# A six-stage transformer kernel on one core: the last value slabs of each mixture layer summed tile by tile over a fourth pair of split buffers, and layer-norm squares centred by half rows

## The chip, the core and the metric

One core of one Trainium2 chip runs the whole program in one launch. The metric is the time on the device in microseconds (us), lower is better; the inputs are random data, batch 1, 256 tokens, width 1024, in f32.

## What is computed

Three mixers alternate with three product-key mixture layers (PEER). The first block (retention mixer, PEER, gated linear recurrence, PEER) closes each stage with a layer norm over a residual, the second (state-space mixer, PEER) with an RMS norm:

```python
h = layer_norm(DN_ALPHA * h + mix, ln_g[layer, 0], ln_b[layer, 0])
ffn = peer(h, peer_w_q[layer], peer_sub_keys[layer], peer_u[layer], peer_v[layer])
h = layer_norm(DN_ALPHA * h + ffn, ln_g[layer, 1], ln_b[layer, 1])
...
h = h + hybrid_mixer(rmsnorm(h, g_mix[l]), ...)
h = h + peer_ffn(rmsnorm(h, g_ffn[l]), ...)
h = rmsnorm(h, g_final)
```

A PEER layer has 16384 experts, of which each token takes 16 for each of 8 heads. The kernel does not gather them: it computes all experts densely, `gelu(x @ u)` times a gate matrix that is zero where an expert was not chosen, times `v`.

## The kernel before

The stages are `ab`, `peer0`, `c`, `peer1`, `s`, `peer2`. Every weight matrix is streamed in **slabs** of 128 x 1024 f32 (512 KB) through three ring buffers (`SLOTS = 3`). Each slab is split into a high and a low part in fp32r, so that three matmuls (high x high, low x high, high x low; L522 to L524, `split_matmuls`) give an f32 product:

- SyncE (`sync_program`, L341) issues the DMA of slab n+3 when the low part of slab n is done (`put`, L344).
- ScalarE copies the slab to `w_hi` (`split_lead`, L764, instruction at L772). It waits for `used`, the count of slabs that TensorE has finished: slab n overwrites the buffers of slab n-3.
- VectorE, in the second half of a PEER layer, or GpSimd elsewhere, computes `w_lo = ring - w_hi` (`split_rest`, L476, instruction at L479).
- TensorE uses it. In a "col" slab (`features`, L536) 24 matmuls of 256 columns produce 128 features in a `col` bank from the transposed input `x_hi`, `x_lo`. In a "row" slab (`rows`, L561) 12 matmuls of 512 columns add to the four banks `acc`, which hold 2 tiles of 128 tokens x 2 halves of 512 columns.

A PEER layer streams 16 query slabs, 128 `u` slabs (features of all experts) and 128 `v` slabs (the values, as rows). For a row slab ScalarE also writes the coefficients `c_hi` (`coef_lead`, L935, instruction at L937) and VectorE `c_lo` (`coef_rest`, L1175, instruction at L1179), again in three buffers. During the value slabs `x_hi` and `x_lo` hold nothing that is read.

**The end of a stage.** `row_tail` (L705) issues the last row slabs. The last but two goes as the others do, all four banks in turn. The last two go by tiles: tile 0 of both slabs, at which `tile_full` is raised; then the left half of tile 1 of both (`tile_full` again), then the right half (`used`). Meanwhile VectorE waits in `add_residual` (L1031), which adds `h` to a bank and, in a layer norm, also takes the sum of the half row. `layer_norm` (L1053) is a hand-written order on VectorE over tiles t and halves: residual, `minus_mean` (needs both halves' sums), `centre` (subtract the mean, times the gain), `variance`, reciprocal (`inverse_std`, L1046), `scale` (L1080; times the inverse deviation plus bias, to `h_tok`). ScalarE does the squares (`centred_squares`, L816; `square`, L826, instruction at L831, with the negated mean of the whole row as its bias), the square root (L814), and then, as TensorE transposes each scaled half (`transpose_x`, L573, 16 matmuls against the identity at L587), the copies to `x_hi` (`lead_x`, L801, L807); VectorE takes `x_lo` (`rest_x`, L1019, L1027). ScalarE's own order is in `finish` (L843), with the `split_lead` of the next stage's first three slabs (`end`, `end + 1`, `end + 2`) put between. The first column matmul of the next stage needs the first half of `x_lo` of both tiles. After `peer1` two norms follow each other, since `s` begins with an RMS norm; `norm_meta` (L1150) norms 16 extra rows before it. `finish_rms` (L1113) is the end of `s` and `peer2`.

## Time and profile before

| | |
|---|---|
| time of the runs, median of 3 | 3011.08 us (3005.74 to 3011.94) |
| time of the profiled execution | 3013.95 us |
| its span | 3012.2 us |
| mean granted TensorE clock | 0.988 of full speed |
| TensorE matmul busy | 2929.7 us (97%) |
| VectorE busy | 2103.5 us (70%) |
| ScalarE busy | 1575.1 us (52%) |
| GpSimd busy | 942.6 us (31%) |
| HBM | 506.05 MB read, 168 GB/s |

The span is that of one profiled execution, on one core; its own time is 1.75 us longer than its span. Engine names in the profile: PE is TensorE, PEld its weight loads, DVE VectorE, ACT ScalarE, POOL GpSimd, SP SyncE. A line such as L522 is a line of the kernel before. Matmuls overlap, so their pitch, from one start to the next, tells more than their length. "[5.00 <-DVE h_tok L1080]" says that the engine sat idle for 5.00 us before the instruction, and that what it waited for was written by VectorE at L1080.

### The profile page before, as it was taken

The page shows a single profiled execution, that of the slowest core. Times are in us where ns is not written, and L with a number is a line of the kernel's source. Part 1 is how long each engine was busy: PE and PEld are TensorE (multiplying, and loading weights), DVE is VectorE, ACT ScalarE, POOL GpSimd, SP SyncE. Part 2 cuts the span into 40 slices and gives each one's busy share as a digit, 9 for nine tenths or more (in the row PEclk, how much of TensorE's full clock was granted, in tenths as well). Part 3 has the DMA queues.
Part 4 walks back from the last instruction along what each step waited for, and adds up shares of the span by engine and source line. Part 5 has one row for each costly group of instructions (what it writes and reads, how often), then busy time and mean ns, then how long its engine had stood idle before and what let it go on. Part 6 is the DMA issues. An engine that isn't in the chain of part 4 may idle for free.

```text
span 3012.2 us, 66185 instructions
## 1 busy us (share of the span) xinstructions
PE 2929.7 (97%) x22893; PEld 2668.0 (89%) x22893; DVE 2103.5 (70%) x4319; ACT 1575.1 (52%) x2604; POOL 942.6 (31%) x378
## 2 busy tenths in 40 slices
PE   7899999999999989999999999899999999999999
PEld 6799999888888879999998888788799999988887
DVE  4369588888655654958888865675629668788755
ACT  3444444577555544454457754553644544477654
POOL 5589600000003757980000000155779810000000
PEclk9999999999999999999999999999999999999999
DMA  5455555555654435555555565444555555555554
GB/s 190 141 169 186 179 165 161 167 166 166 219 191 162 152 112 171 184 183 160 166 163 166 166 213 196 147 131 123 156 172 180 184 168 165 164 165 166 185 193 162
DMA packets 142993, 508.68 MB, mean 169 GB/s; under 512 B 17168, under 2 KB 18192, under 8 KB 142880
## 3 DMA queue, kind: packets, MB, share of 16 engines
q1 hardware_dynamic: 142880, 507.16, 52.4%
q8 instruction: 72, 1.18, 0.2%
q14 instruction: 41, 0.34, 0.0%
HBM read 506.05 MB, written 1.05 MB: 168 GB/s over the span
## 4 chain that ended last, share of the span: by engine, by line
PE 89%; DVE 5%; POOL 2%; ACT 2%; issue 1%; DMA 1%; SPq 0%; DVEq 0%; ACTq 0%; POOLq 0%
PE col L522 15%; PE col L524 15%; PE col L523 15%; PE acc L522 12%; PE acc L524 12%; PE acc L523 12%; POOL w_lo L479 2%; PE acc L645 2%; PE col L645 2%; ACT w_hi L772 1%; PE acc L605 1%; DMA ring<-in_ab_in 1%; DVE work L1838 0%; DVE work L1546 0%; DVE work L2294 0%
## 5 line engine op out<-in xcount | busy, mean ns | idle before, releaser
L479 POOL TENSOR_TENSOR w_lo<-ring,w_hi 128x1024 fp32r<-128x1024 f32 x374 | 942.4, 2530 | 1482.9 <-ACT w_hi L772 1481.8
L772 ACT ACTIVATE w_hi<-ring 128x1024 fp32r<-128x1024 f32 x941 | 993.7, 1056 | 556.9 <-PE acc L524 454.5
L522 PE MATMUL col<-x_hi,w_hi 128*128 128x256 f32 (+1 forms) x3976 | 1133.3, 285 | 10.8 <-DVE x_lo L1027 7.0
L523 PE MATMUL col<-x_lo,w_hi 128*128 128x256 f32 (+1 forms) x3976 | 1122.6, 282 | 0.0
L524 PE MATMUL col<-x_hi,w_lo 128*128 128x256 f32 (+1 forms) x3976 | 1121.5, 282 | 0.0
L479 DVE TENSOR_TENSOR w_lo<-ring,w_hi 128x1024 fp32r<-128x1024 f32 x567 | 693.2, 1223 | 261.7 <-ACT w_hi L772 260.6
L522 PEld LDWEIGHTS col<-x_hi,w_hi 128*128 128x128 f32 x3976 | 754.5, 190 | 16.5 <-issue 11.4
L524 PEld LDWEIGHTS col<-x_hi,w_lo 128*128 128x128 f32 x3976 | 755.5, 190 | 0.0
L523 PEld LDWEIGHTS col<-x_lo,w_hi 128*128 128x128 f32 x3976 | 751.9, 189 | 0.7
L522 PE MATMUL acc<-w_hi,c_hi 128*128 128x512 f32 x1664 | 660.8, 397 | 9.4 <-DVE c_lo L1172 5.3
L524 PE MATMUL acc<-w_hi,c_lo 128*128 128x512 f32 x1664 | 650.1, 391 | 0.0
L523 PE MATMUL acc<-w_lo,c_hi 128*128 128x512 f32 x1664 | 648.8, 390 | 0.0
L779 ACT ACTIVATE work<-col 128x256 f32 (+1 forms) x464 | 178.8, 385 | 775.1 <-PE col L524 774.9
L522 PEld LDWEIGHTS acc<-w_hi,c_hi 128*128 128x128 f32 x1664 | 313.3, 188 | 74.9 <-DVE c_lo L1172 6.6
L524 PEld LDWEIGHTS acc<-w_hi,c_lo 128*128 128x128 f32 x1664 | 313.0, 188 | 67.4
L523 PEld LDWEIGHTS acc<-w_lo,c_hi 128*128 128x128 f32 x1664 | 313.7, 189 | 62.5
L1298 DVE TENSOR_TENSOR gated_onehot_i<-mask_i,pairs_of_gate 128x768 bf16<-128x768 bf16 x384 | 227.9, 594 | 12.3
L1179 DVE TENSOR_TENSOR c_lo<-work,c_hi 128x256 fp32r<-128x256 f32 x387 | 163.7, 424 | 1.6 <-ACT c_hi L937 1.5
L937 ACT ACTIVATE c_hi<-work 128x256 fp32r (+1 forms) x384 | 153.4, 401 | 5.9 <-DVE work L1308 5.9
L1186 DVE MAX8 work<-work 128x8 f32<-128x128 f32 (+1 forms) x144 | 35.4, 322 | 168.4 <-ACT work L893 168.1
L1288 DVE TENSOR_TENSOR mask_i<-iota_bf,pairs_of_i_i 128x256 bf16<-128x256 bf16 x384 | 121.3, 316 | 44.5 <-DVE gated_onehot_i L1298 41.7
L1308 DVE TENSOR_TENSOR work<-work,acc 128x256 f32 (+1 forms) x192 | 73.9, 421 | 100.3 <-PE acc L645 55.4
(287 smaller groups left out, 2099.9 us busy)
## 6 DMA issues: line engine op xcount, KB each, us to landing
ring<-in_u SPq DMA_DIRECT2D x384, 512.0 KB, 3.5
ring<-in_v SPq DMA_DIRECT2D x384, 512.0 KB, 3.6
ring<-in_wq SPq DMA_DIRECT2D x48, 512.0 KB, 3.5
ring<-in_s_in SPq DMA_DIRECT2D x21, 512.0 KB, 3.6
ring<-in_c_in SPq DMA_DIRECT2D x16, 512.0 KB, 3.5
ring<-in_s_out SPq DMA_DIRECT2D x16, 512.0 KB, 3.6
ring<-in_s_gate SPq DMA_DIRECT2D x12, 512.0 KB, 3.5
ring<-in_s_conv SPq DMA_DIRECT2D x12, 512.0 KB, 3.6
```

Of the source, the lines that this page charges most:

```text
L479: eng.tensor_tensor(k.w_lo[s.slot][:, :], k.ring[s.slot][:, :], k.w_hi[s.slot][:, :].bitcast(F32), ALU.subtract).then_inc(k.lo[s.slot], 1)
L522: pe.matmul(out, a[0], b[0], start=start, stop=False, **kw)
L523: pe.matmul(out, a[0], b[1], start=False, stop=False, **kw)
L524: return pe.matmul(out, a[1], b[0], start=False, stop=stop, **kw)
L645: ins = pe.matmul(banks[b.slot][:, t * EARLY:(t + 1) * EARLY], k.oh1[:, b.base % 2, t, :], k.oh2[:, b.base % 2, n, t, :], start=n == 0, st ...
L772: act.activation(k.w_hi[s.slot][:, :], k.ring[s.slot][:, :], ACT.Copy).then_inc(k.hi[s.slot], 1)
L779: act.activation(dst, src, func).then_inc(k.evac, 1)
L937: act.activation(k.c_hi[s.slot][:, :], act_of[:, s.index(values), :], ACT.Copy).then_inc(k.coef_h, 1)
L1179: dve.tensor_tensor(k.c_lo[s.slot][:, :], src, k.c_hi[s.slot][:, :].bitcast(F32), ALU.subtract).then_inc(k.coef[s.slot], 1)
L1288: dve.tensor_tensor(mask, pairs[:, at // 2:(at + EARLY) // 2, :].unsqueeze(1).to_broadcast(shape), k.i2[:, tokens, :].unsqueeze(2).to_broa ...
L1298: dve.tensor_tensor(k.oh2[:, slot, :, :, :].rearrange("p n t (i two) -> p n t i two", two=2), mask.unsqueeze(1).to_broadcast(shape), k.gat ...
L1308: dve.tensor_tensor(part, part, banks[b.slot][:, 0:GB * EARLY].rearrange("p (t i) -> p i t", t=GB), ALU.mult).then_inc(k.g_used, 1)
```

## The change

Four things are changed.

1. **Buffers.** In each PEER layer the last 12 value slabs (`DEEP`) use four pairs of split buffers: the three `w_hi`/`w_lo` and a fourth in `x_hi`/`x_lo`. A slab there overwrites that of four before it. ScalarE and VectorE split slab n+1 ahead of the coefficients of slab n; the last slab's coefficients go to a further piece of `x_hi`/`x_lo`.
2. **Tail.** In a PEER layer the last four slabs go by tiles (`LONG`) and no longer the last two: tile 0 of all four, then the left half of tile 1 of all four, then the right half. At the end of a mixer it is two slabs as before (`SHORT`).
3. **Squares.** ScalarE squares each half row about the half's own mean, so that it needs the sum of that half alone. VectorE corrects the variance by the distance of the two half means, with two more small instructions for a tile (`mean` has two where `minus_mean` had one, and there is `apart`).
4. **Order.** `layer_norm`, `finish_rms` and `finish` are written in another order: tile 0 is brought to its scaled rows earlier, and the residual of tile 1's right half comes behind that in a PEER layer. `mean_square` has one instruction where it had two; RMS_EPS is the bias of the square root.

```diff
+SHORT, LONG = 2, 4
+DEEP = 3 * LONG
...
+    def open_deep(self):
+        self.w_home, self.w_before, self.c_home = {}, {}, {}
+        spare = [t[:, :, :].rearrange("p c t -> p (c t)") for t in (self.x_hi, self.x_lo)]
...
+            homes = [[t[:, 0:D] for t in spare]] + [[self.w_hi[n % SLOTS][:, :], self.w_lo[n % SLOTS][:, :]]
+                                                    for n in range(deep - SLOTS, deep)]
+            for n in range(DEEP):
+                self.w_home[deep + n] = homes[n % LONG]
+                self.w_before[deep + n] = deep + n - LONG if n else None
+            self.c_home[end - 1] = [t[:, D:D + T] for t in spare]
...
     def row_tail(self, end, count):
+        tail = [Slab(n) for n in range(end - count, end)]
...
+        for s in tail:
+            pe.wait_ge(k.coef[s.slot], k.rows_in_slot(s, 1))
+            self.slab_ready(s)
             for half in range(2):
+                ins = part(s, 0, half)
         ins.then_inc(k.tile_full, 1)
+        for s in tail:
+            ins = part(s, 1, 0)
+        ins.then_inc(k.tile_full, 1)
+        for s in tail:
+            part(s, 1, 1).then_inc(k.used, 1)
...
     def split_lead(self, s):
+        if s.turn is None and s.base in k.w_home:
+            if k.w_before[s.base] is not None:
+                act.wait_ge(k.used, k.w_before[s.base] + 1)
+        elif s.turn is not None or s.base >= SLOTS:
             act.wait_ge(k.used, s.index(SLOTS - 1))
...
     def finish(self, name, end):
+        deep = name[:4] == "peer"
...
+        if not deep:
+            self.split_lead(Slab(end))
+        for half in range(2):
+            self.centred_square(0, half)
+        self.tile_std(0, eps)
+        self.centred_square(1, 0)
+        if deep:
+            self.split_lead(Slab(end))
         if after != ("s",):
+            if deep:
+                self.split_lead(Slab(end + 1))
+                self.lead_x([0], halves=[0])
+                self.centred_square(1, 1)
+                self.tile_std(1, eps)
+                self.lead_x([0], halves=[1])
+            else:
+                self.centred_square(1, 1)
+                self.split_lead(Slab(end + 1))
+                self.tile_std(1, eps)
+                self.lead_x([0])
             self.lead_x([1])
             self.split_lead(Slab(end + 2))
         else:
+            self.tile_squares(0)
+            self.split_lead(Slab(end + 1))
+            self.centred_square(1, 1)
             self.tile_std(1, eps)
             self.lead_meta()
+            self.tile_squares(1)
+            self.split_lead(Slab(end + 2))
             self.lead_x(range(NT), at=META)
...
     def peer(self, layer):
+        self.split_lead(Slab(values + deep - 1))
+        for n in range(deep - 1, KEYS):
+            if n + 1 < KEYS:
+                self.split_lead(Slab(values + n + 1))
             coef_lead(Slab(values + n))
...
     def layer_norm(self, slot, last, rms_next, deep):
         residual(0, 0)
         residual(0, 1)
-        minus_mean(0)
-        residual(1, 0)
+        mean(0)
         centre(0, 0)
-        residual(1, 1)
-        minus_mean(1)
+        apart(0)
+        if not deep:
+            residual(1, 0)
         centre(0, 1)
         variance(0)
-        centre(1, 0)
-        centre(1, 1)
-        variance(1)
-        own.join()
+        residual(1, 0 if deep else 1)
+        if not deep:
+            mean(1)
         self.inverse_std(0)
         scale(0, 0)
         scale(0, 1)
+        if rms_next:
+            self.mean_square(0, squared + 5)
+        if deep:
+            residual(1, 1)
+            mean(1)
+        if rms_next:
+            self.inverse_std(0)
+        centre(1, 0)
+        apart(1)
+        variance(1)
+        centre(1, 1)
+        own.join()
         self.inverse_std(1)
         scale(1, 0)
+        scale(1, 1)
...
     def finish_rms(self, name, last):
+        residual(0, 0)
+        residual(0, 1)
+        if not deep:
+            residual(1, 0)
+        self.mean_square(0, squared + 2)
+        if not deep:
+            residual(1, 1)
+        self.inverse_std(0)
+        self.rms_norm(0, slot)
+        if deep:
+            residual(1, 0)
+            residual(1, 1)
+        self.mean_square(1, squared + 4)
+        self.inverse_std(1)
+        self.rms_norm(1, slot)
```

The order of instructions on VectorE at the end of `peer0`, from the last coefficients on, before:

```order
L1179 TENSOR_TENSOR c_lo<-work,c_hi 128x256
L1039 SCALAR_TENSOR_TENSOR acc,small<-h_tok,acc 128x512 x2
L1063 TENSOR_SCALAR small<-small 128x1
L1039 SCALAR_TENSOR_TENSOR acc,small<-h_tok,acc 128x512
L1071 SCALAR_TENSOR_TENSOR acc<-acc,small,work 128x512
L1039 SCALAR_TENSOR_TENSOR acc,small<-h_tok,acc 128x512
L1063 TENSOR_SCALAR small<-small 128x1
L1071 SCALAR_TENSOR_TENSOR acc<-acc,small,work 128x512
L1075 TENSOR_SCALAR small<-small 128x1
L1071 SCALAR_TENSOR_TENSOR acc<-acc,small,work 128x512 x2
L1075 TENSOR_SCALAR small<-small 128x1
```

and now (L1093 is the residual, L1116 and L1117 the mean, L1123 the centring, L1128 `apart`, L1134 the variance, L1101 the reciprocal, L1139 the scaling):

```order
L1260 TENSOR_TENSOR c_lo<-work,c_hi 128x256
L1260 TENSOR_TENSOR x_lo<-work,x_hi 128x256
L1093 SCALAR_TENSOR_TENSOR acc,small<-h_tok,acc 128x512 x2
L1116 TENSOR_SCALAR small<-small 128x1
L1117 TENSOR_SCALAR small<-small 128x1
L1123 SCALAR_TENSOR_TENSOR acc<-acc,small,work 128x512
L1128 SCALAR_TENSOR_TENSOR small<-small 128x1
L1123 SCALAR_TENSOR_TENSOR acc<-acc,small,work 128x512
L1134 TENSOR_SCALAR small<-small 128x1
L1093 SCALAR_TENSOR_TENSOR acc,small<-h_tok,acc 128x512
L1101 RECIPROCAL small<-small 128x1
L1139 SCALAR_TENSOR_TENSOR h_tok<-acc,small,work 128x512 x2
```

Tile 0 runs through to its scaled rows with only one residual of tile 1 among it, where before both residuals and both centrings of tile 1 stood ahead of the first scaling.

The order on ScalarE at the same place, from the last slab's split on, before:

```order
L772 ACTIVATE w_hi<-ring 128x1024
L937 ACTIVATE c_hi<-work 128x256
L847 ACT_TABLE_LOAD
L847 ACTIVATE small<-small 128x1
L772 ACTIVATE w_hi<-ring 128x1024
L831 ACTIVATE work,small<-acc,small 128x512 x4
L814 ACTIVATE small<-small 128x1 x2
L772 ACTIVATE w_hi<-ring 128x1024
L807 ACTIVATE x_hi<-acc 128x4x128 x4
L772 ACTIVATE w_hi<-ring 128x1024
```

and now (L809 is a slab's high part, L988 the coefficients, L868 a square, L851 a square root, L844 the copy to `x_hi`):

```order
L809 ACTIVATE w_hi<-ring 128x1024
L988 ACTIVATE c_hi<-work 128x256
L988 ACTIVATE x_hi<-work 128x256
L886 ACT_TABLE_LOAD
L886 ACTIVATE small<-small 128x1
L868 ACTIVATE work,small<-acc,small 128x512 x2
L851 ACTIVATE small<-small 128x1
L868 ACTIVATE work,small<-acc,small 128x512
L809 ACTIVATE w_hi<-ring 128x1024 x2
L844 ACTIVATE x_hi<-acc 128x4x128
L868 ACTIVATE work,small<-acc,small 128x512
L851 ACTIVATE small<-small 128x1
```

The square root of tile 0 stands after two squares, no longer after four. The splits of the next stage's first two slabs and a copy to `x_hi` stand ahead of the last square.

## Rows read from the trace of the kernel before

**Rows 1.** The page: the chain that ended last, by engine.
```profile
PE 89%; DVE 5%; POOL 2%; ACT 2%; issue 1%; DMA 1%; SPq 0%; DVEq 0%; ACTq 0%; POOLq 0%
```

**Rows 2.** Timeline, PE, end of peer0: start us, us, engine, line, op, xcount, [idle <-releaser].
```profile
939.81 0.39 PE L523 MATMUL acc<-w_lo,c_hi 128*128 128x512 f32 x1
940.04 0.39 PE L524 MATMUL acc<-w_hi,c_lo 128*128 128x512 f32 x1
...
945.43 3.67 PE L587 MATMUL acc<-ident,h_tok 128*128 128x128 f32 x16 [5.00 <-DVE h_tok L1080]
...
949.75 0.36 PE L522 MATMUL col<-x_hi,w_hi 128*128 128x256 f32 x1 [0.65 <-DVE x_lo L1027]
```

**Rows 3.** Timeline, DVE, layer norm at the end of peer0.
```profile
937.75 0.70 DVE L1039 SCALAR_TENSOR_TENSOR acc<-h_tok,acc 128x512 f32<-128x512 f32 x1 [2.79 <-PE acc L524]
...
938.36 0.73 DVE L1039 SCALAR_TENSOR_TENSOR acc<-h_tok,acc 128x512 f32<-128x512 f32 x1
...
939.18 0.21 DVE L1063 TENSOR_SCALAR small<-small 128x1 f32<-128x1 f32 x1
...
940.31 0.76 DVE L1071 SCALAR_TENSOR_TENSOR acc<-acc,small,work 128x512 f32<-128x512 f32 x1 [0.25 <-issue]
...
944.62 1.41 DVE L1080 SCALAR_TENSOR_TENSOR h_tok<-acc,small,work 128x512 f32<-128x512 f32 x2
...
946.14 1.41 DVE L1080 SCALAR_TENSOR_TENSOR h_tok<-acc,small,work 128x512 f32<-128x512 f32 x2
...
948.91 1.89 DVE L1027 TENSOR_TENSOR x_lo<-acc,x_hi 128x512 fp32r<-128x512 f32 x3 [0.77 <-ACT x_hi L807]
```

**Rows 4.** Timeline, ACT, the same stretch.
```profile
939.43 0.69 ACT L831 ACTIVATE work<-acc,small 128x512 f32<-128x512 f32 x1 [3.29 <-DVE small L1063]
...
944.74 1.04 ACT L772 ACTIVATE w_hi<-ring 128x1024 fp32r<-128x1024 f32 x1
...
948.28 0.60 ACT L807 ACTIVATE x_hi<-acc 128x512 fp32r<-128x512 f32 x1 [0.26 <-PE acc L587]
```

**Rows 5.** Timeline, ACT and DVE, last value slabs of peer0.
```profile
932.31 1.06 ACT L772 ACTIVATE w_hi<-ring 128x1024 fp32r<-128x1024 f32 x1 [1.28 <-PE acc L524]
...
933.40 1.23 DVE L479 TENSOR_TENSOR w_lo<-ring,w_hi 128x1024 fp32r<-128x1024 f32 x1 [1.08 <-ACT w_hi L772]
934.54 0.42 DVE L1179 TENSOR_TENSOR c_lo<-work,c_hi 128x256 fp32r<-128x256 f32 x1
```

**Rows 6.** Windows: stretch, us, busy (xinstructions) of PE, PEld, DVE, ACT, POOL, PEclk, DMA share, GB/s.
```profile
949.80:954.50 4.70, 4.70 (x40) 4.70 (x41) 3.73 (x9) 3.39 (x4) 2.41 (x1) 1.00 0.27 104
1944.90:1949.40 4.50, 4.50 (x20) 4.50 (x21) 1.50 (x5) 0.00 (x0) 0.00 (x0) 0.50 0.01 4
2183.60:2188.30 4.70, 4.70 (x23) 4.70 (x23) 0.76 (x2) 0.84 (x1) 3.18 (x2) 0.50 0.47 146
2190.40:2195.10 4.70, 4.70 (x42) 4.70 (x41) 0.00 (x0) 2.06 (x4) 4.27 (x2) 1.00 0.28 93
```

**Rows 7.** Timeline, ACT, DVE and PE, end of peer1.
```profile
1924.56 1.28 ACT L847 ACT_TABLE_LOAD   x1
...
1928.96 0.68 DVE L1039 SCALAR_TENSOR_TENSOR acc<-h_tok,acc 128x512 f32<-128x512 f32 x1
...
1942.28 1.97 PE L587 MATMUL acc<-ident,work 128*128 128x128 f32 x8 [0.18 <-DVE work L1146]
1944.90 0.56 PE L522 MATMUL col<-x_hi,w_hi 128*128 128x272 f32 x1 [0.65 <-DVE x_lo L1027]
```

**Rows 8.** Timeline, PE, end of stage s.
```profile
2181.08 1.78 PE L587 MATMUL acc<-ident,work 128*128 128x128 f32 x8 [0.82 <-DVE work L1146]
```

**Rows 9.** Timeline, DVE, the last of the kernel.
```profile
3002.62 2.05 DVE L1039 SCALAR_TENSOR_TENSOR h_tok<-h_tok,acc 128x512 f32<-128x512 f32 x3 [2.79 <-PE acc L524]
...
3007.46 0.15 DVE L1131 TENSOR_TENSOR small<-small 128x1 f32<-128x1 f32 x1
...
3008.27 1.42 DVE L1146 SCALAR_TENSOR_TENSOR work<-h_tok,small,work 128x512 f32<-128x512 f32 x2
```

More of the change, by code:

```diff
@@ L236, in __init__, with w_at, c_at @@
             "s_ydiag", "s_ysum", "s_z", "s_zc", "s_zsilu", "s_gated", "s_msq", "s_y", "s_yT", "s_y_ready")}
+    def open_deep(self):
+        self.w_home, self.w_before, self.c_home = {}, {}, {}
+        spare = [t[:, :, :].rearrange("p c t -> p (c t)") for t in (self.x_hi, self.x_lo)]
+        for layer in range(3):
+            if f"v{layer}" not in self.first:
+                continue
+            end = self.first[f"v{layer}"] + KEYS
+            deep = end - DEEP
+            homes = [[t[:, 0:D] for t in spare]] + [[self.w_hi[n % SLOTS][:, :], self.w_lo[n % SLOTS][:, :]]
[4 more added lines that the diff above has]
+            self.c_home[end - 1] = [t[:, D:D + T] for t in spare]
+    def w_at(self, s):
+        if s.turn is None and s.base in self.w_home:
+            return self.w_home[s.base]
+        return self.w_hi[s.slot][:, :], self.w_lo[s.slot][:, :]
+    def c_at(self, s):
+        if s.turn is None and s.base in self.c_home:
+            return self.c_home[s.base]
+        return self.c_hi[s.slot][:, :], self.c_lo[s.slot][:, :]
     def cols(self, s):
@@ L693, in peer @@
         self.row_slab(Slab(first + BATCHES))
-        with pe.Fori(0, VREST // SLOTS - 1) as i:
+        with pe.Fori(0, (VREST - DEEP) // SLOTS) as i:
             for p in range(SLOTS):
                 self.row_slab(Slab(first + BATCHES + 1 + p, i))
-        self.row_tail(first + KEYS)
+        for n in range(KEYS - DEEP, KEYS - LONG):
+            self.row_slab(Slab(first + n))
+        self.row_tail(first + KEYS, LONG)
     def row_slab(self, s, start=False, stop=False):
@@ L799, in lead_meta, with lead_x @@
                             ACT.Copy).then_inc(k.xhi, 1)
-    def lead_x(self, tiles, at=0):
+    def lead_x(self, tiles, at=0, halves=(0, 1)):
         k, act, w = self.k, self.act, self.w
         for t in tiles:
-            for half in range(2):
+            for half in halves:
                 w.next(k.xt)
@@ L814, in std, with centred_square, square @@
         act.activation(dst, src, ACT.Sqrt, bias=bias).then_inc(k.std, 1)
-    def centred_squares(self, t):
+    def centred_square(self, t, half):
         k = self.k
-        self.w.next(k.mean)
-        for half in range(2):
-            self.square(k.acc[t * 2 + half][:, :], 2 * t + half, bias=k.small[:, 20 + t:21 + t])
+        self.w.next(k.summed)
+        n = 2 * t + half
+        self.square(k.acc[n][:, :], n, bias=k.small[:, 16 + n:17 + n], scale=-512.0)
     def tile_std(self, t, bias=0.0):
         self.std(self.k.small[:, 4 + t:5 + t], self.k.small[:, 8 + t:9 + t], bias)
-    def square(self, src, n, bias=0.0):
+    def square(self, src, n, bias=0.0, scale=1.0):
         k, act, rows, cols = self.k, self.act, src.shape[0], src.shape[1]
@@ L1107, in layer_norm @@
             self.rest_meta()
+            self.inverse_std(1)
             self.rms_norm(1, 2)
+            self.w.skip(k.sq, 8)
         else:
-            scale(1, 1)
             self.w.skip(k.h_part, 4)
+            self.w.skip(k.sq, 4)
+        self.w.skip(k.summed, 4)
     def finish_rms(self, name, last):
-        slot = 0 if name == "s" else 1
-        for t in range(NT):
-            for half in range(2):
-                if t and half:
-                    self.mean_square(0)
-                self.add_residual(t, half, last, 1.0, saved=True)
@@ new lines, in finish_rms, with residual @@
+        slot, squared = 0 if name == "s" else 1, self.w.count(k.sq)
+        def residual(t, half):
+            self.add_residual(t, half, last, 1.0, saved=True)
+        residual(0, 0)
[6 more added lines that the diff above has]
+        self.inverse_std(0)
+        self.rms_norm(0, slot)
+        if deep:
+            residual(1, 0)
+            residual(1, 1)
+        self.mean_square(1, squared + 4)
@@ L1137, in rms_norm, with mean_square @@
+        self.inverse_std(1)
+        self.rms_norm(1, slot)
+        self.w.skip(k.sq, 4)
+    def mean_square(self, t, squares):
+        k, dve = self.k, self.dve
+        dve.wait_ge(k.sq, squares)
+        first, second = k.small[:, 40 + 2 * t:41 + 2 * t], k.small[:, 41 + 2 * t:42 + 2 * t] if t < NT else 0.0
+        dve.tensor_scalar(k.small[:, 4 + t:5 + t], first, second, 1.0 / D, ALU.add, ALU.mult).then_inc(k.var, 1)
     def rms_norm(self, t, slot):
         k, dve = self.k, self.dve
-        self.inverse_std(t)
@@ L1152, in norm_meta @@
         k = self.k
-        self.mean_square(NT)
+        self.w.skip(k.sq, 1)
+        self.mean_square(NT, self.w.count(k.sq))
         self.inverse_std(NT)
@@ L1386, in vector_program @@
     e.own.do(dve.memset(k.small[:, 49:50], LN_EPS))
+    e.own.do(dve.memset(k.small[:, 50:51], RMS_EPS))
     dve.wait_ge(k.const, 32)
```

138 lines of the change are left out of this document (56 added, 82 removed).

## The prediction, made before the changed kernel was run

> **What bounds the kernel now.** I read the chain of waits first. TensorE holds 89% of it and VectorE 5% [rows 1]: the kernel is matmuls, with short breaks where a stage ends. So I then read the PE timeline at the end of each stage. At the end of `peer0` the last row matmul starts at 940.04, the transposes at 945.43 after 5.00 us of idle time, the first column matmul at 949.75 [rows 2]. The ends of `ab` and `c` look the same. Row matmuls start 0.23 apart (0.227 over the whole run of them), so a slab of 12 takes 2.72, and the change takes no matmul away. All it can do is begin the norm earlier and shorten it; five breaks between stages and the last norm are at stake. The DVE and ACT timelines [rows 3, 4] show what fills a break: VectorE begins the first residual at T = 937.75, scales tile 0 from T+6.87 and tile 1 from T+8.39, and columns begin at T+12.00. Last, the windows show the granted clock where columns begin [rows 6]: 1.00 after `peer0` (2.4 GHz), but 0.50 (1.2 GHz) for 4.5 us after `peer1` and 4.7 us after `s`.
>
> **The tail (three PEER layers).** With four slabs by tiles, tile 0 is complete two slabs of half work earlier: the second half of four slabs is 5.44 us before the end, that of two was 2.72. T moves forward by 2.72. Against that stands a new wait. Coefficients and splits of the last slabs are wanted sooner. For the last but one, ScalarE may start when the slab three before it is done, at a time I call B; before, TensorE reached that slab at B+5.44, now at B+2.72, since the two slabs between give only their tile 0. The present work from there: the high part starts 0.20 behind B (932.31 against a slab that starts at 932.11, which is 940.04+0.23 less three slabs), VectorE's low part at B+1.29, `c_lo` at B+2.43 and 0.42 long [rows 5], done at B+2.85. The change keeps that order (split of the next slab, then coefficients). That is 0.13 late; with the restart of the matmuls I take 0.3 a layer. The bounds are 0, if the split runs ahead of its wait, and 1.1, a whole split by ScalarE [rows 5] in the way. So T' = T-2.72+0.30 = T-2.42. The other eight slabs in the fourth pair only run ahead, cost nothing, and hide behind 2.72 of matmuls a slab, against 1.06+0.40 on ScalarE and 1.65 on VectorE.
>
> **peer0's norm, from T'.** Residuals start 0.61 apart, a scaling 0.66 behind the one before (two took 1.41) [rows 3]; I take 0.15 for a small instruction, 0.2 where it waits. Tile 0: residuals 0 and 0.61, two means at 1.43, centring 1.85 (the first square now waits for its own residual alone, and is done by 1.6), `apart`, second centring 2.66, variance 3.44, residual of tile 1 left 3.58, reciprocal 4.36, scaling 4.56 and 5.22. Tile 1: its last residual, queued behind these, 5.88, though TensorE would release it at 5.44; means to 7.0, centring 7.05. ScalarE comes to the last square only behind two splits of next slabs (1.04 each [rows 4]) and one copy to `x_hi`: start 7.6, done 8.4. Variance 8.43, second centring, reciprocal 9.37, scaling from 9.57. TensorE transposes tile 1's left half at 10.4; a copy follows 1.15 behind (945.43 to the first copy, as four transposes at the low clock took), then `x_lo` 0.63 and columns 0.84 behind that [rows 2 to 4]: T'+13.0. The norm itself is thus 1.0 longer (13.0 against 12.0), and the layer's gain is 2.42-1.0 = **-1.4**. POOL and SP: the split of slab `end` now comes some 9 us later on ScalarE, so POOL's low part and the DMA of slab `end + 3` behind it move with it, to some 10 us before that slab is copied. That is hidden; without the cover it would be at most 3.5, one landing.
>
> **ab and c (two norms, tail unchanged).** T stays. By the same pitches: centring 1.85, residual of tile 1 left 2.64, centring 3.25, variance 4.0, last residual 4.17, means 4.95, reciprocal 5.35, scaling 5.55; then centring 6.87 and 7.9 with two small ones between, reciprocal 8.7, scaling 8.9. So tile 0 is scaled at T+5.55 instead of 6.87, but tile 1 at T+8.9 instead of 8.39, because four small instructions are added and nothing that was on VectorE's path leaves it. Before, tile 1 waited for TensorE in any case: 12 transposes in a row, copy at T+10.53 [rows 4]. Now T+8.9+0.75+0.06+1.15 = T+10.86: **+0.3** each. The Trainium skill, VectorE: DVE Perf Modes, section Rules for kernel authors, speaks against this part: minimise the count of chained instructions, not semaphores. Counted so, four at 0.15 would be +0.6 each, and the sum 0.6 worse.
>
> **peer1.** VectorE's first residual at 1928.96 stood 4.40 behind ScalarE's table load at 1924.56 [rows 7], for the extra rows' norm. The load follows the last coefficients and moves by some 2.35 (2.72, less 0.37 for one pair of coefficients more behind the same split), so T' = 1926.6. But the residual of tile 1's right half now queues behind the mean square of tile 0, which needs two more squares: it comes 7.7 behind the first. By the same counting columns come at T'+17.85 = 1944.45, against 1944.90: **-0.45**.
>
> **s and the last norm.** One small instruction less in the mean square of tile 1, 0.19 with its wait [rows 9]: **-0.2** after `s`. The last norm: tile 0 is done early, residual of tile 1's right half at T'+5.44, then its square 6.16 (0.73 with its sum), mean square 6.9, root 7.1, reciprocal 7.3, scaling 7.5 and 8.17, its end at T'+8.92. Before it was 3002.62+7.07 [rows 9]. So 8.92-2.42-7.07 = **-0.57**.
>
> Sum: -1.4+0.3+0.3-0.45-0.2-0.57 = **-2.0 us**.
>
> **The clock.** This can outweigh it. After `ab`, `peer0` and `c` all 16 transposes ran in one block (3.67 [rows 2]) right up to the columns, and these began at 1.00. After `s` the transposes had a hole of 0.82 [rows 8], and columns stayed at 0.50 for 4.7 us: 23 matmuls, where 42 fit at the full clock [rows 6]. 19 at 4.70/42 = 0.112 are 2.1 us lost. After `peer1` the hole was only 0.18 [rows 7], and the clock was low too. The change opens holes of 2 to 3 us between the tiles' transposes in all three good breaks. I take one of the three to lose 2.1: **+2.1**; bounds are none and all three. The Trainium skill, TensorE: Matmul & The Clock Gate, section Part 1, says that the throttled state is the default and that sustained activity releases it. By that rule all three would lose: the sum would be +4.3. The trace agrees after `s`, not plainly after `peer1`.
>
> Total: -2.0+2.1 = +0.1, against the profiled execution's 3013.95 gives 3014.0. The median of the runs lies 2.87 lower; so does my number: **3011.1**.
>
> **The rivals.**
> - *Only the chain moves.* Clocks fall as now: -2.0, 3009.1. For it: three of five breaks began fast, though the clock had fallen in between. Chance 0.2.
> - *Slower: the clock stays low in all three broken blocks.* -2.0+6.3 = +4.3, 3015.4. The place is the first 4 to 5 us of columns after `ab`, `peer0` and `c`; the price 2.1 each. From one loss on it cancels the gain, from four (with a longer tail wait) it passes 0.2%. Chance 0.2.
> - *Faster: the early transposes keep the clock up.* They follow the row matmuls within a microsecond, where 5 us of idle time stood. Then `peer1` and `s` lose nothing either: -2.0-4.2 = -6.2, and shorter transposes: 3004.5. Against it: nearly 4 us idle remain. Chance 0.12.
> - *The change doesn't do what it says.* TensorE waits 2.4 in each tail for the last slabs' parts, so that T stays. Then -2.0+3x2.42 = +5.3, 3016.4. The rows give 0.1 late, so 0.03.
> - The forecast, one break slow: 0.45.
>
> **How the numbers follow.** A measurement of this kernel tells 0.2%, 6.0 us, from no change; the runs shown spread over 6.2. Faster is most of the third rival and the edge of the first: 0.13. Slower is the upper part of the second and the fourth: 0.07. The range reaches from 3004 (third rival) to 3016 (second, near the fourth).
>
> **What would show it.** Right: in PEER layers the first residual 5.2 before the last row matmul is issued out, where it was 2.5 (940.27 less 937.75); a wait of TensorE of 0.2 to 0.4 for `c_lo` in each tail; columns after `peer0` 10.6 behind the old T, after `ab` and `c` 12.3; transposes in two blocks. Wrong: waits over 1 us in the last 12 slabs, columns after `peer0` less than 1 us earlier, or the clock at 1.00 (or 0.50) at all five starts.

## The result: 3021.3 us against 3011.9, slower by 0.32%

| | before | after |
|---|---|---|
| median of 7 runs each, us | 3011.85 | 3021.32 |
| range, us | 3005.74 to 3015.72 | 3016.29 to 3025.31 |
| profiled execution, us (its span) | 3013.95 (3012.2) | 3021.34 (3019.5) |
| ratio | | 1.0032 [1.0022, 1.0042] |

The forecast was 3011.1, no change, with a range from 3004 to 3016. The measured time lies above the range, and the interval of the ratio lies wholly above 1. On the page of the changed kernel the totals hardly move; the chain has one per cent less of TensorE and one more of VectorE than before [rows 1]:

```profile
PE 2934.0 (97%) x22893; PEld 2669.5 (88%) x22893; DVE 2109.7 (70%) x4330; ACT 1574.7 (52%) x2604; POOL 941.9 (31%) x378
...
PE 88%; DVE 6%; POOL 2%; ACT 2%; issue 1%; DMA 0%; SPq 0%; DVEq 0%; ACTq 0%; POOLq 0%
```

The longest pieces of the chain name what was not there before: one VectorE instruction on a 128x1 tile, once after `ab` and once after `c` (columns: start us, us on the chain, what).

```profile
116.35 1.92 DVE small L1128
...
1110.93 1.92 DVE small L1128
```

L1128 is `apart`, the new small instruction (gap squared plus the squares' sum). The VectorE timeline after `ab` shows it between the first centring of tile 1 and its variance:

```profile
115.60 0.75 DVE L1123 SCALAR_TENSOR_TENSOR acc<-acc,small,work 128x512 f32<-128x512 f32 x1
116.26 2.00 DVE L1128 SCALAR_TENSOR_TENSOR small<-small 128x1 f32<-128x1 f32 x1
118.37 0.21 DVE L1134 TENSOR_SCALAR small<-small 128x1 f32<-128x1 f32 x1
118.50 0.75 DVE L1123 SCALAR_TENSOR_TENSOR acc<-acc,small,work 128x512 f32<-128x512 f32 x1
```

and GpSimd's timeline of the same stretch the split of the slab after next:

```profile
115.90 2.34 POOL L511 TENSOR_TENSOR w_lo<-ring,w_hi 128x1024 fp32r<-128x1024 f32 x1 [6.38 <-ACT w_hi L809]
```

One element a partition takes 2.00 us, and ends at 118.26, where GpSimd's subtraction ends (115.90+2.34 = 118.24). For tile 0, with GpSimd idle, the same instruction took 0.21.

TensorE after `ab` (the first row is the last row matmul; the columns begin at 122.91), then after `peer0`:

```profile
111.02 0.39 PE L555 MATMUL acc<-w_hi,c_lo 128*128 128x512 f32 x1
115.08 1.31 PE L618 MATMUL acc<-ident,h_tok 128*128 128x128 f32 x8 [3.67 <-DVE h_tok L1139]
120.29 1.97 PE L618 MATMUL acc<-ident,h_tok 128*128 128x128 f32 x8 [3.89 <-DVE h_tok L1139]
122.91 0.55 PE L553 MATMUL col<-x_hi,w_hi 128*128 128x256 f32 x1 [0.65 <-DVE x_lo L1081]
...
944.37 0.39 PE L555 MATMUL acc<-w_hi,x_lo 128*128 128x512 f32 x1
944.60 1.27 PE L618 MATMUL acc<-ident,h_tok 128*128 128x128 f32 x8
949.92 1.97 PE L618 MATMUL acc<-ident,h_tok 128*128 128x128 f32 x8 [4.05 <-DVE h_tok L1139]
952.54 0.55 PE L553 MATMUL col<-x_hi,w_hi 128*128 128x256 f32 x1 [0.65 <-DVE x_lo L1081]
```

The block of 16 transposes [rows 2] is broken in two. The first 4.5 us of columns behind `ab`, `peer0`, `c`, `peer1` and `s` (windows; of each the time and matmuls of PE first, then PEld, DVE, ACT, POOL, the granted clock, the DMA share and GB/s):

```profile
122.80:127.30 4.50, 4.39 (x22) 4.42 (x23) 1.16 (x2) 1.03 (x2) 2.37 (x1) 0.56 0.44 150
952.50:957.00 4.50, 4.46 (x24) 4.49 (x25) 3.71 (x9) 3.19 (x5) 2.37 (x1) 0.58 0.13 51
1117.40:1121.90 4.50, 4.41 (x21) 4.44 (x22) 1.14 (x2) 1.01 (x2) 2.36 (x1) 0.50 0.44 150
1954.70:1959.20 4.50, 4.44 (x19) 4.47 (x20) 1.56 (x5) 0.04 (x1) 0.26 (x1) 0.50 0.36 117
2193.00:2197.50 4.50, 4.46 (x38) 4.49 (x39) 1.09 (x2) 2.04 (x3) 3.50 (x2) 1.00 0.50 156
```

Where [rows 6] had 1.00 behind `peer0` there is now 0.58, and behind `ab` and `c` 0.56 and 0.50, with 22 and 21 matmuls in place of about 40. Behind `s` it is the other way round: 1.00 where 0.50 was, though nothing in that break changed by more than 0.05 us.

For all comparisons I take two marks from each trace. F is the start of the last row matmul plus its 0.23. The first mark is the start of the columns behind F, the second the start of the matmul 300 further on, which has the clock's loss in it too.

| behind | columns, before | after | 300 on, before | after | low clock from the first column on, before | after |
|---|---|---|---|---|---|---|
| `ab` | 9.49 | 11.66 | 44.85 | 48.73 | 0 | 3.89 |
| `peer0` | 9.48 | 7.94 | 45.49 | 45.18 | 0 | 3.70 |
| `c` | 9.49 | 11.66 | 44.85 | 49.70 | 0 | 6.00 |
| `peer1` | 13.76 | 14.70 | 58.86 | 59.84 | 4.54 | 5.00 |
| `s` | 6.18 | 6.13 | 43.80 | 41.49 | 5.06 | 0 |
| `peer2` (end of the program) | 7.02 | 6.35 | | | | |

The second marks move by +3.88, -0.31, +4.85, +0.98 and -2.31, the end of the program by -0.67, and the three long stretches from a second mark to the F of a PEER layer's end grow by +0.53, +0.09 and +0.58 (the wait in the tail is in them). Together that is +7.6; the two profiled executions differ by 7.4, and the rest, -0.2, lies in the other stretches. `ab` and `c` alone lose 8.7.

### The profile page after: what moved, and what is told of

Read it like the earlier page. It is cut to its first block, busy times and chain, and to the rows that moved or that the text cites. A ratio compares the mean times of both kernels' runs of the same rounds, so it can differ in the third digit from the quotient of the medians.

```text
span 3019.5 us, 65949 instructions
## 1 busy us (share of the span) xinstructions
PE 2934.0 (97%) x22893; PEld 2669.5 (88%) x22893; DVE 2109.7 (70%) x4330; ACT 1574.7 (52%) x2604; POOL 941.9 (31%) x378
## 4 chain that ended last, share of the span: by engine, by line
PE 88%; DVE 6%; POOL 2%; ACT 2%; issue 1%; DMA 0%; SPq 0%; DVEq 0%; ACTq 0%; POOLq 0%
PE col L553 15%; PE col L555 15%; PE col L554 15%; PE acc L553 12%; PE acc L555 12%; PE acc L554 12%; PE acc L676 2%; POOL w_lo L511 2%; PE col L676 2%; PE acc L636 1%; ACT w_hi L809 1%; DMA ring<-in_ab_in 0%; DVE work L1923 0%; DVE work L2379 0%; DVE c_lo L1252 0%
## 5 line engine op out<-in xcount | busy, mean ns | idle before, releaser
L809 ACT ACTIVATE w_hi<-ring 128x1024 fp32r<-128x1024 f32 x932 | 984.2, 1056 | 540.4 <-PE acc L555 427.8
L553 PE MATMUL col<-x_hi,w_hi 128*128 128x256 f32 (+1 forms) x3976 | 1135.2, 286 | 10.6 <-DVE x_lo L1081 7.0
L511 DVE TENSOR_TENSOR w_lo<-ring,w_hi 128x1024 fp32r<-128x1024 f32 x558 | 681.6, 1222 | 246.9 <-ACT w_hi L809 245.4
L553 PE MATMUL acc<-w_hi,c_hi 128*128 128x512 f32 x1616 | 642.5, 398 | 9.1 <-DVE c_lo L1252 5.0
L555 PE MATMUL acc<-w_hi,c_lo 128*128 128x512 f32 x1616 | 631.7, 391 | 0.0
L554 PE MATMUL acc<-w_lo,c_hi 128*128 128x512 f32 x1616 | 630.2, 390 | 0.0
L553 PEld LDWEIGHTS acc<-w_hi,c_hi 128*128 128x128 f32 x1616 | 304.2, 188 | 74.2 <-DVE c_lo L1252 6.3
L555 PEld LDWEIGHTS acc<-w_hi,c_lo 128*128 128x128 f32 x1616 | 304.1, 188 | 65.9
L554 PEld LDWEIGHTS acc<-w_lo,c_hi 128*128 128x128 f32 x1616 | 304.6, 188 | 60.4
L988 ACT ACTIVATE c_hi<-work 128x256 fp32r (+1 forms) x381 | 152.2, 401 | 5.9 <-DVE work L1388 5.9
```

Source lines behind the costliest of these rows:

```text
L511: eng.tensor_tensor(lo, k.ring[s.slot][:, :], hi.bitcast(F32), ALU.subtract).then_inc(k.lo[s.slot], 1)
L553: pe.matmul(out, a[0], b[0], start=start, stop=False, **kw)
L554: pe.matmul(out, a[0], b[1], start=False, stop=False, **kw)
L555: return pe.matmul(out, a[1], b[0], start=False, stop=stop, **kw)
L809: act.activation(k.w_at(s)[0], k.ring[s.slot][:, :], ACT.Copy).then_inc(k.hi[s.slot], 1)
L988: act.activation(k.c_at(s)[0], act_of[:, s.index(values), :], ACT.Copy).then_inc(k.coef_h, 1)
```

## The experiments

Each kernel had 11 or 12 runs beside the kernel before on the same chip (the one with half rows alone had 5); its ratio is to the kernel before.

**1. `apart` in another form.** The instruction reads two SBUF tensors and a per-partition scalar; here it reads one tensor and two scalars.

```diff
-own.do(dve.scalar_tensor_tensor(k.small[:, 28 + t:29 + t], gap, gap, k.small[:, 40 + 2 * t:41 + 2 * t],
+own.do(dve.tensor_scalar(k.small[:, 28 + t:29 + t], gap, gap, k.small[:, 40 + 2 * t:41 + 2 * t],
                          ALU.mult, ALU.add))
```

> The small instruction that adds the squared gap to the sum of squares (apart) gets one tensor operand and two per-partition scalars where it had two tensor operands and one scalar; all else is the changed kernel. Theory A (an instruction of VectorE that reads two operands from SBUF waits until GpSimd's subtraction of two SBUF operands is over): apart for tile 1 takes 0.2 us where it took 2.00 (ab, c), 1.00 (peer0) and 1.78 (peer1); columns after ab and c begin 9.9 us behind the start F of the last row matmul's end instead of 11.66, and the whole is some 5 us faster than the changed kernel: 3016, ratio to before 1.0015. Rival B (the instruction waits for something else that comes late, such as the sum of the square, whatever its form): apart stays at 2.0 us, 3021.

**2. `apart` as it is, GpSimd's work moved.** In `finish`, after `ab` and `c`:

```diff
 self.centred_square(1, 1)
-self.split_lead(Slab(end + 1))
 self.tile_std(1, eps)
+self.split_lead(Slab(end + 1))
 self.lead_x([0])
```

> Only after ab and c: ScalarE splits the slab after next behind the root of tile 1, not ahead of it, so that GpSimd's low part is not under way while apart runs; apart keeps its two tensor operands. Theory A: apart for tile 1 takes 0.2 us after ab and c and stays at 1.0 and 1.8 after peer0 and peer1; columns after ab and c some 1.8 us earlier, 3017.5 in all. Rival B (the form of the instruction is slow here, or it waits for ScalarE's square): it stays at 2.0 us and the time at 3021.

Measured: 3013.5 us, 1.0009 [1.0000, 1.0018] for the first, 3018.5 us, 1.0022 [1.0013, 1.0031] for the second. All eight `apart` of each (times in ns: least, median, most), first kernel and then second:

```profile
L1128 DVE TENSOR_SCALAR small<-small x8: 263/265/266, 106.4 to 1937.4; 128x1 f32<-128x1 f32 x8
```

```profile
L1128 DVE SCALAR_TENSOR_TENSOR small<-small x8: 207/210/1779, 111.9 to 1943.1; 128x1 f32<-128x1 f32 x8
```

In the second kernel `apart` of tile 1 after `ab` took 0.21 (116.99), GpSimd's subtraction starting only at 118.87; after `peer1`, where nothing was moved, the 1.78 remains. In the first, GpSimd worked from 111.12 to 113.47 and `apart` at 111.48 took 0.27 all the same. Either changing the form or taking GpSimd's work away removes the wait: theory A holds, B falls. The Trainium skill, SBUF — State Buffer, section Who interferes with whom, says so: an instruction of VectorE with two SBUF inputs contends with one of GpSimd that reads SBUF, and the later one is blocked, not slowed. The traces agree: 2.00 us for one element a partition. Columns begin at F+9.97 and F+9.87 after `ab`, for 11.66. But in both, 5.7 and 5.8 us of the columns behind it are still at the low clock. In the whole, the new form of this one instruction takes 7.9 us off the changed kernel's median, most of the 9.5 that the change had cost; that is more than the 5 that were expected.

**3. The norms after `ab` and `c` as before, PEER layers changed.** `layer_norm` and `finish` take the old order, mean and squares where the stage is not a PEER layer.

> The norms after ab and c get back the order, the mean and the squares of the kernel before; the PEER layers keep the change. Theory (the two short norms carry the loss, 4.4 us each in the first 300 matmuls behind them): columns after ab and c begin 9.5 us behind F at the full clock, the time falls by 8.7 to 3012.5, within 0.1% of the kernel before. Rival (the loss is spread over the program, as by the longer unrolled code or the state of the clock in general): it falls by less than 4.

Measured: 3010.3 us, 1.0001 [0.9992, 1.0010]. Columns there at F+9.29 and F+9.48, low clock 0. Its median is 11 us below the changed kernel's, but its runs lie in two groups (3008.3 to 3010.3 and 3014.2 to 3015.2) with the median at the edge of the lower one; by the means it is 8.8, which is what `ab` and `c` had lost. What the PEER layers bring with the change is not seen in the time: after `peer0` columns come at F+7.49, but with 5.2 us of low clock.

**4. Half rows without the tail.** `row_tail` of two slabs and the short norms' order in all stages of the changed kernel (`deep = False`, `SHORT` for `LONG`).

> The changed kernel with the tail of two slabs in the PEER layers too, and the order of the short norms everywhere: the half-row squares alone. Theory (the squares by half rows, with their longer line of small instructions and the broken block of transposes, are what costs): peer0 and peer1 then lose as ab and c do, some 4 us more each than the changed kernel or half of it, 3023 to 3028. Rival (the tail with its unrolled slabs is what costs): below 3018.

Measured: 3023.5 us, 1.0039 [1.0026, 1.0053]. After `peer0` columns begin at F+11.66 with 3.9 us of low clock, as after `ab`; after `peer1` at 15.54. So the half rows as they are written, `apart` in its first form included, cost the time, and not the tail. (The time itself can't be told from the changed kernel's, 1.0032; the marks carry the reading.)

**5. The tail without half rows.** The other half of the change on the kernel before, with ScalarE's `split_lead(Slab(end))` of the PEER layers behind the squares of tile 0.

> The kernel before with the change's tail alone: four slabs by tiles and the fourth pair of buffers in the PEER layers, ScalarE's split of the next slab behind the squares of tile 0; VectorE's order, the mean and the squares as before. Theory (the tail moves the first residual 2.4 us forward, but in the old order the first centring stands behind the residual of tile 1's left half, which the tail frees only 2.7 us behind tile 0, so that little of it is left): columns behind peer0 at F+9.0 to 9.5, time 3010 to 3011.5. Rival (the tail is a gain by itself): 2 us less in each of three layers, 3005.5.

Measured: 3013.1 us, 1.0005 [0.9995, 1.0014]. Columns after `peer0` at F+8.99, after `peer1` 13.48, last norm unchanged at 7.02. The time is a little above what was expected. The tail alone gives 0.5, of which 0.3 is paid for the wait in the tail. So it needs a new order of VectorE. Whether that order can be had with the squares about the whole row's mean, without the half rows' small instructions, no run shows. (In this kernel 3.5 us behind `peer0` were at the low clock, though all 16 transposes ran in one block.)

**6. TensorE kept busy.** Matmuls without a use between the transposes; for the first such kernel:

```diff
+FILL = {'peer0': (16, 18), 'c': (0, 19), 'peer1': (16, 18)}
...
+    def keep(self, n):
+        for _ in range(n):
+            self.pe.matmul(self.k.misc[:, 0:P], self.k.ident[:, :], self.k.ident[:, :], start=True, stop=True)
...
         for t in range(NT):
+            self.keep(fill[t])
```

> Matmuls of 128x128 without a use fill TensorE's idle time: 16 before the transposes of tile 0 and 18 before those of tile 1 after ab and c, 19 before those of tile 1 after peer0; they write a bank that nobody reads. Theory C (the hole between the two tiles' transposes keeps the clock at 1.2 GHz into the columns: 3.9, 3.7 and 6.0 us of low clock there): the low stretches there are gone, columns begin some 0.5 earlier, and the time is 6 to 8 us below the changed kernel, 3014. Rival D (the clock there is chance, or the matmuls come too late to hold it): low stretches stay, 3021; if a filler takes over 0.25 us, columns begin later and it is slower.

Measured: 3016.8 us, 1.0018 [1.0009, 1.0027], 4.6 below the changed kernel where 6 to 8 were expected. After `ab` (one filling matmul is about two records, 0.23 us):

```profile
111.82 3.62 PE L607 MATMUL misc<-ident 128*128 128x128 f32 x31
115.54 1.32 PE L624 MATMUL acc<-ident,h_tok 128*128 128x128 f32 x8
116.69 4.18 PE L607 MATMUL misc<-ident 128*128 128x128 f32 x36
120.75 1.31 PE L624 MATMUL acc<-ident,h_tok 128*128 128x128 f32 x8
122.91 0.36 PE L554 MATMUL col<-x_hi,w_hi 128*128 128x256 f32 x1 [0.84 <-DVE x_lo L1087]
```

Low clock is gone behind `ab`, `peer0` and `c`; 300 matmuls on, `ab` and `c` are 2.2 and 3.2 better than in the changed kernel (46.57, 46.53). `peer0` is not (45.63 for 45.18), although its columns begin 0.4 earlier and at the full clock: TensorE then waits 2.6 us for the low part of the fourth slab. That wait is taken up again below.

**7. One block, or one hole?** First the 16 transposes after `ab` and `c` held until the left half of tile 1 is scaled (cheap `apart`), then eight filling matmuls in the hole between the tiles alone (cheap `apart`).

```diff
-pe.wait_ge(k.h_part, parts - 4 + 2 * t + half + 1)
+pe.wait_ge(k.h_part, parts - 4 + (max(3, 2 * t + half + 1) if name in ("peer0", "peer1") else
+                                  2 * t + half + 1))
```

> The kernel with the cheap form of apart, and after ab and c the transposes of tile 0 wait until the left half of tile 1 is scaled, so that all 16 run in one block. Theory C (the hole between the transposes keeps the clock low): columns after ab and c begin 1.6 us later, F+11.6 for 9.97, but at the full clock (low stretch in them 0 for 5.7 and 5.0), and 300 matmuls on they are even or 0.5 to 0.9 ahead: 3012.5. Rival D (the clock falls there whatever the transposes do): low stretch as long as before and 1.6 later each, 3016.7.

```diff
+FILL = {'peer0': (0, 8), 'peer1': (0, 8)}
```

> The changed kernel with the cheap apart and 8 filling matmuls between the two tiles' transposes after ab and c alone; the first idle stretch (3.9 us, before tile 0's transposes) stays as it is. Theory E (the full clock comes back a few microseconds after TensorE works again without a hole, so what counts is when that begins: F+3.9 in place of F+7.36): low stretches in the columns after ab and c shrink from 5.7 and 5.0 us to between 0 and 3, time 3010 to 3011.5. Rival (any idle stretch of 3.9 us ahead of the columns costs the same, or the return is chance): they stay at 4 to 6, 3013.5.

Measured: 3014.6 us, 1.0011 [1.0002, 1.0021], and 3014.3 us, 1.0008 [0.9998, 1.0017]; both the same as experiment 1 within the interval, and both above what was expected (3012.5, and 3010 to 3011.5). The first 4.5 us of columns behind `ab` and `c`, one block:

```profile
118.40:122.90 4.50, 4.50 (x24) 4.50 (x25) 1.03 (x2) 0.91 (x1) 2.37 (x1) 0.57 0.13 32
1112.80:1117.30 4.50, 4.49 (x38) 4.50 (x39) 1.06 (x2) 2.27 (x3) 2.40 (x1) 1.00 0.12 35
```

and the hole filled:

```profile
121.65:126.15 4.50, 4.50 (x38) 4.50 (x39) 1.04 (x2) 1.89 (x3) 2.40 (x1) 1.00 0.41 141
1115.10:1119.60 4.50, 4.50 (x38) 4.50 (x39) 1.04 (x2) 1.89 (x3) 2.40 (x1) 1.00 0.47 148
```

The same block of 3.7 us right up to the columns was followed by the low clock once and by the full one once, in one execution: an unbroken block is not enough. What sorts the breaks of all profiled executions behind `ab`, `peer0` and `c` without filling ahead of tile 0 is how long before the columns TensorE began to work again without a hole. The last hole ends 2.1 to 2.7 us ahead of them wherever the block is broken (as in the changed kernel): low clock in all 15 such breaks, 3.0 to 6.0 us of it. It ends 4.3 ahead where the 16 transposes run together: full clock in 8 of 10. With the hole filled it is 6.7 (F+3.9 to F+10.56), and both breaks are at the full clock, although the clock had fallen before and the eight matmuls, at half speed, took 3.6 us for 1.9 and put the columns 0.6 later. So the marks are as theory E has them, and C holds in a weaker form: what the hole seems to take away is the head start. That is an ordering of these breaks, not a cause shown. The filled hole is two breaks of one execution, and `peer1` and `s` are not in the count: with only short idle stretches in their last 5 and 4 us (0.13 to 0.18 and about 0.8) they began at the full clock in 4 of 10 and 6 of 10 traces without filling, the same instructions giving either. Chance has a part that these runs don't separate. 300 matmuls on, filling the hole is 2.0 and 1.6 better than experiment 1 (45.93, 45.92 for 47.89, 47.53). The time as a whole did not follow: in that profiled execution `peer0` and `peer1` had 3.0 and 4.1 us of low clock, and how much of that the median holds stays open.

**8. Filled breaks, with and without the change.** Norms after `ab` and `c` as before, PEER layers changed, cheap `apart`, `FILL = {"peer0":(21,0), "c":(0,15), "peer1":(21,0), "s":(32,0), "peer2":(6,3)}`; and the kernel before with 21, 21, 21, 33 and (6, 3). They write a column's bank in place of `misc`.

> Norms after ab and c as in the kernel before, PEER layers as changed, apart in the cheap form, and TensorE's idle time at all five breaks filled with 128x128 matmuls without a use (21 after ab and c, 15 between the tiles after peer0, 32 behind the extra rows' transposes after peer1, 6 and 3 after s). Theory: on top of the kernel with the old norms after ab and c (3010.3) 0.5 at ab and c, 1.8 and 2.2 at peer1 (apart, clock), 2.4 at s: 3003. Rival (fed too fast, columns wait for GpSimd's low parts, 2.4 us a slab, and for the chain of small instructions ahead of the third slab's split): 3006 or more, waits of 1 to 3 us in the first slabs behind the breaks.

> The kernel before, nothing changed but the same filling matmuls in its five breaks (21, 21, 21, 33 behind the extra rows' transposes, 6 and 3). Theory C: no low clock at any start of columns, 0.5 us from faster transposes at the first three, 2.3 after peer1 and 2.5 after s: 3005.5, ratio 0.998. It is what the clock is worth without the change. Rival D: no change, 3011.5.

Measured: 3006.9 us, 0.9983 [0.9974, 0.9992], and 3009.0 us, 0.9995 [0.9986, 1.0004], for 3003 and 3005.5 expected. The first beats both kernels; the wait that its rival expected is there, 2.58 between two starts at the fourth slab of `c`. The second can't be told from the kernel before. In it all five breaks end at 1.00, 300 matmuls behind `ab`, `c`, `peer1` and `s` are 0.7, 0.7, 2.8 and 2.3 ahead, but `peer0` is 2.9 behind (48.43 for 45.49). VectorE, GpSimd, ScalarE and TensorE at the start of `c` in that kernel:

```profile
949.81 2.27 DVE L1820 TENSOR_TENSOR work<-work 128x8 f32<-128x8 f32 x1
952.45 1.76 DVE L1821 MEMSET work<- 128x2048 f32 x1 [0.38 <-issue]
...
949.65 2.40 POOL L480 TENSOR_TENSOR w_lo<-ring,w_hi 128x1024 fp32r<-128x1024 f32 x1 [1.69 <-ACT w_hi L778]
...
954.46 0.21 ACT L1757 ACTIVATE work<-work 128x16 f32<-128x16 f32 x1 [3.58 <-DVE work L1823]
...
959.89 0.53 PE L523 MATMUL col<-x_hi,w_hi 128*128 128x256 f32 x1 [2.29 <-POOL w_lo L480]
```

The same contention, in code that the change does not touch: a 128x8 maximum of two SBUF tensors, 0.16 long in the kernel before, falls into GpSimd's subtraction here and takes 2.27. In the kernel before it started at 950.72, 0.04 ahead of GpSimd's (950.76), and was not held; here it starts at 949.81, 0.16 behind it. ScalarE's exponential, then its split of the fourth slab, then GpSimd's low part stand behind it, and 2.57 us lie between the starts of two matmuls.

**9. The chain at the start of `c` shortened.** In the vector program of `c`, in both kernels of experiment 8:

```diff
 own.do(dve.tensor_tensor(self.max, self.bound[:, 0, :], self.bound[:, 1, :], ALU.max))
-own.do(dve.memset(self.probs, 0.0))
 own.join()
 dve.tensor_tensor(self.exps, self.bound, self.max.unsqueeze(1).to_broadcast([P, 2, CH]), ALU.subtract)\
    .then_inc(m["c_lb"], 1)
+own.do(dve.memset(self.probs, 0.0))
```

> The fastest kernel so far (old norms after ab and c, cheap apart, filled breaks, 3006.9) with one line moved: VectorE's memset of 1.76 us at the start of c goes behind the subtraction that ScalarE's exponential waits for. Theory (after peer0 the gain of the earlier columns is held back by this chain: small instructions of VectorE, the exponential, then ScalarE's split and GpSimd's low part of the fourth slab, for which TensorE waits 2.58 us): the wait falls by 2.1 to about 0.5, 300 matmuls behind peer0 come at F+43.2 for 45.24, and the time is 3004.8. Rival (TensorE waits for GpSimd's own pace of 2.4 us a slab or for the transfers): the wait moves to the next slabs, 3006.9.

> The kernel before with the filled breaks and VectorE's memset at the start of c moved as in the fastest kernel: the same as that one but for the change's tail and norms in the PEER layers. Theory (with the clock kept and the chain at the start of c shortened, the PEER part of the change is worth its share: columns 1.7 us earlier after peer0, 0.2 after peer1, 0.7 in the last norm): 3007, some 2.5 above the fastest kernel; 300 matmuls behind peer0 at F+46.3 for 43.14. Rival (it is worth nothing there, and the gain was all clock and memset): 3004.5.

Measured: 3004.3 us, 0.9981 [0.9972, 0.9990], and 3007.9 us, 0.9986 [0.9977, 0.9995]. In the first of them:

```profile
943.57 2.28 DVE L1979 TENSOR_TENSOR work<-work 128x8 f32<-128x8 f32 x1
945.88 0.17 DVE L1981 TENSOR_TENSOR work<-work 128x16 f32<-128x16 f32 x1
...
951.57 0.36 PE L555 MATMUL col<-x_hi,w_hi 128*128 128x256 f32 x1 [0.20 <-POOL w_lo L513]
```

The contention is still there (2.28), but the memset no longer stands behind it, and the 2.58 between the starts of two matmuls are down to 0.48. 300 matmuls behind `peer0` come at F+43.14, as expected, for 44.84 in the second kernel: there the PEER part of the change is worth 1.7, and 0.7 in the last norm, before the 0.3 in each tail. In the whole the medians differ by 3.5, the means by 2.6, with intervals that overlap; how much the PEER part is worth in time stays open. This is the fastest kernel, 0.19% below the one before. In the second kernel the filling did not hold the clock behind `peer1`: it fell to 0.50 1.7 us ahead of the columns, and 5.1 us of them ran so, where the same filling in experiment 8 had none.

## Why the prediction was wrong

**The sum of the chain, -2.0.** The step that failed is "I take 0.15 for a small instruction, 0.2 where it waits". It took the price of a small instruction from rows where GpSimd was idle [rows 3], and asked nowhere what GpSimd does beside it, although the order of the change puts ScalarE's splits, and GpSimd's work behind them, into that place. What the runs showed instead: `apart` of tile 1 took 2.00 us, because it waited for GpSimd's subtraction (experiments 1 and 2). `apart` of tile 1 waited 1.79 more than tile 0's after `ab` and `c`, 0.8 after `peer0`, and after `peer1` 1.5 more than in experiment 1: 5.9 in all, against a forecast gain of 2.0. Without it (experiment 2 for `ab` and `c`, 1 for the rest, each with 0.3 for the tail in the PEER layers) the terms measure:

| term | forecast | with the port wait | without |
|---|---|---|---|
| `ab`, `c` | +0.3 each | +2.17 each | +0.38 each |
| `peer0` | -1.4 | -1.24 | -2.06 |
| `peer1` | -0.45 | +1.24 | -0.23 |
| `s`, last norm | -0.2, -0.57 | -0.05, -0.37 | -0.04, -0.37 |
| sum | -2.0 | +3.9 | -1.9 |

So the working by pitches was right to 0.7 us a term, and to 0.1 in the sum, where `peer0` came 0.7 better and the other terms together 0.7 worse, which is luck; one instruction was wrong. `ab` and `c` would have been a small loss in any case.

**The tail.** The step of 2.72, less 0.3 for the new wait, was right. The first residual stands 5.24 ahead of F at the ends of `peer0` and `peer2`, where it stood 2.52, and 4.83 at `peer1`, where it stood 2.19. TensorE waits twice, 0.18 and 0.11, for the last slabs' `c_lo`. Experiment 5 shows that the tail is worth almost nothing alone. Of the signs that the prediction named, columns after `peer0` came where it said (10.5 behind the old T, for 10.6), after `ab` and `c` they did not (14.2 for 12.3).

**The clock, +2.1.** "I take one of the three to lose 2.1" is the second step that failed, in its size: all three good breaks lost, 3.9, 3.7 and 6.0 us at half speed. That is the rival "slower: the clock stays low in all three broken blocks" (chance 0.2), with its place right. Its price was a little high at `ab` (1.7 beyond the later columns) and low at `c` (2.7). At `peer0` it was 1.2, but that could not be had back by the clock alone: with the clock held (experiment 6), TensorE waited for the fourth slab instead, and was no earlier. The reason given, the broken block, fits all fifteen broken blocks of experiment 7's count; what in it matters is argued there, not shown. The Trainium skill's rule that I set beside it (TensorE: Matmul & The Clock Gate, Part 1) had the outcome right, and would have given more than my number.

**The cover over the next slabs.** "That is hidden" held for slab `end + 3`'s transfer. But the fourth slab's low part hangs on VectorE's first instructions of the next stage too, and the prediction had no term for that chain; before the change two starts there lay 0.51 us apart already, in experiments 6 and 8 it was 2.58. In the changed kernel no two lie over 0.35 apart: its slow columns come to the fourth slab later. The gain of `peer0` came out as 0.3 after 300 matmuls, where columns were 1.5 earlier.

The sum by what was measured: +3.9 on the chain and +5.6 for the clock behind `ab`, `peer0` and `c` (1.7+1.2+2.7) is +9.5, the difference of the medians. That leaves the -2.3 behind `s` as luck of the two profiled executions: the low clock is there in 4 of 10 traces with the same break. Over all runs there is the mean granted clock of each (three digits). Twice what it lacks of 1, times the span, is the time at the low clock: 79 us in a run of the changed kernel (7 runs), 66 in the kernel before (33 runs), 64 in experiment 3. The 13 more are of the size that the columns after `ab`, `peer0` and `c` show (3.9+3.7+6.0). The slower rival, +4.3, had the clock but not the blocked instruction, and the range ended at 3016.

## What to carry to other kernels

A small VectorE instruction is cheap only if it cannot be blocked: before one is added to a chain that TensorE waits for, look at what GpSimd does in that stretch, and give it at most one SBUF tensor (per-partition scalars cost 0.27 beside GpSimd, two tensors up to 2.00). When a wait is shortened, read the first slabs behind it as well: what bounded the break comes back three slabs on. And read the granted clock behind a break as well as its length: work done earlier, with a hole of 1.6 us or more behind it, bought no clock in any of 15 breaks here.

## What the runs showed that was not expected

- A 128x1 instruction took 2.00 us and a 128x8 one 2.27 us beside a 128x1024 subtraction on GpSimd, each ending within 0.03 us of it. GpSimd's own instruction was not slowed measurably (2.34 beside `apart`, 2.36 without). Where VectorE is first, it is GpSimd's that is long: after `peer1` in the changed kernel VectorE's 128x512 scaling of two SBUF tensors (L1225, two from 1951.33, 1.42 together) was under way when GpSimd's subtraction began at 1952.12, and that took 2.84.
- Filling matmuls held the full clock over idle stretches of 1.6 to 8 us in 22 of 23 breaks; the one exception is `peer1` of the last kernel. They cost nothing where they ended before the data came, and 0.6 us where the clock had already fallen (0.45 us each for 0.23).
- Behind `s` the columns began at the low clock in four profiled executions and at the full one in six of those without filling, with the same instructions in the break and the columns at F+6.13 to F+6.19.
- Part of the spread of every kernel lies in the first stage, which the change touches only at its end. In the 14 profiled executions the F of `ab` is at 106.4 to 106.8 us in four, with 6.8 us of low clock before it, and at 111.0 to 112.6 in the other ten, with 13.7 to 20.5. So the time of one profiled execution can be 5 us off another's for this alone, and marks counted from F are free of it.
